# A chunk's 21 projection steps in two runs instead of five, inside a delta-rule recurrence

## The reference

```
def step(s, inp):
    r_t, w_t, k_t, v_t, kk_t, a_t = inp
    sa = einsum('bhij,bhj->bhi', s, -kk_t)
    s = s * w_t + sa (kk_t * a_t) + v_t k_t
    return s, einsum('bhij,bhj->bhi', s, r_t)
```

## Time and profile before

| what | value |
|---|---|
| median of 3 runs | 1475.15 us (1470.92 to 1475.57) |
| the profiled execution's own time | 1467.87 us |
| its span (first to last instruction) | 1466.2 us |
| TensorE busy | 1438.5 us, 98% of the span |
| VectorE busy | 837.8 us, 57% |
| ScalarE busy | 409.4 us, 28% |
| GpSimd busy | 184.5 us, 13% |
| mean granted TensorE clock | 0.997 |

### The profile page before, as it was taken

The page is one execution under the profiler, slowest core; times in us unless marked ns, Lnnn a source line. Parts: engine busy times, 40 slices in busy tenths (PEclk is TensorE's granted clock), DMA queues, the critical chain, the costliest instruction groups (busy, mean ns, idle before and its releaser), DMA issues.

```text
span 1466.2 us, 30386 instructions
## 1 busy us (share of the span) xinstructions
PE 1438.5 (98%) x12380; PEld 1138.4 (78%) x12380; DVE 837.8 (57%) x1634; ACT 409.4 (28%) x888; POOL 184.5 (13%) x256
## 2 busy tenths in 40 slices
PE   9999999999999999999999999999999999999997
PEld 8887578878888866886668668888788888888886
DVE  7665058633433446315774537677666766666664
ACT  3112372123233215216775631102211011101001
POOL 1000324532222212205001310000000000000000
PEclk9999999999999999999999999999999999999999
DMA  6222543211111247447001974422222222222221
GB/s 264 87 87 72 181 167 114 93 61 46 47 47 42 95 160 233 148 132 237 32 2 53 325 297 147 140 94 87 73 86 86 75 84 87 85 73 97 90 86 61
DMA packets 57399, 163.94 MB, mean 112 GB/s; under 512 B 7312, under 2 KB 19696, under 8 KB 55952
## 3 DMA queue, kind: packets, MB, share of 16 engines
q1 hardware_dynamic: 48608, 121.46, 25.2%
q0 software_dynamic: 7936, 39.40, 7.6%
q10 hardware_dynamic: 720, 1.16, 0.2%
HBM read 144.01 MB, written 22.15 MB: 113 GB/s over the span
## 4 chain that ended last, share of the span: by engine, by line
PE 93%; DVE 3%; ACT 1%; issue 1%; DMA 0%; SPq 0%; DVEq 0%; ACTq 0%
PE acc L1049 26%; PE acc L1194 14%; PE acc L1980 5%; PE acc L2008 5%; PE acc L1989 5%; PE acc L1219 5%; PE acc L2033 4%; PE acc L1142 2%; PE acc L1335 2%; PE acc L1157 2%; PE acc L1735 2%; PE acc L1747 2%; PE acc L1631 1%; PE acc L1758 1%; PE acc L1352 1%; PE acc L1061 1%
## 5 line engine op out<-in xcount | busy, mean ns | idle before, releaser
L1049 PE MATMUL acc<-sb_work,sb_ring 128*128 128x272 f32 x602 | 150.8, 392 | 0.0
L2530 ACT ACTIVATE sb_omemT<-acc 128x272 f32<-128x272 f32 x74 | 29.3, 396 | 386.1 <-PE acc L1980 234.5
L1049 PE MATMUL acc<-sb_work 128*128 128x272 f32 x530 | 133.0, 393 | 0.0
L1049 PEld LDWEIGHTS acc<-sb_work,sb_ring 128*128 128x128 f32 x602 | 114.4, 190 | 23.6
L1049 PEld LDWEIGHTS acc<-sb_work 128*128 128x128 f32 x530 | 100.5, 190 | 21.4 <-issue 0.8
L1194 PE MATMUL acc<-sb_work,sb_ring 128*128 128x272 f32 x360 | 93.3, 399 | 2.9 <-DVE sb_work L2739 2.9
L1194 PEld LDWEIGHTS acc<-sb_work,sb_ring 128*128 128x128 f32 x360 | 66.4, 190 | 17.9 <-issue 4.4
L1980 PE MATMUL acc<-sb_work,sb_ring 128*128 128x272 f32 x308 | 77.2, 393 | 1.0 <-issue 1.0
L1219 PE MATMUL acc<-sb_work,sb_ring 128*128 128x272 f32 x320 | 77.7, 395 | 0.0
L1989 PE MATMUL acc<-sb_work,sb_ring 128*128 128x272 f32 x308 | 77.1, 392 | 0.0
L1219 PEld LDWEIGHTS acc<-sb_work,sb_ring 128*128 128x128 f32 x320 | 59.7, 190 | 14.9 <-issue 3.3
(11 more groups left out here) (491 smaller groups left out, 2771.9 us busy)
## 6 DMA issues: line engine op xcount, KB each, us to landing
sb_ring<-w_stream SPq DMA_DIRECT2D x144, 512.0 KB, 3.5
sb_work<-pages SPq DMA_DIRECT2D x56, 192.0 KB, 4.2
branch_gates<-sb_work SPq DMA_DIRECT2D x24, 272.0 KB, 2.7
sb_work<-branch_gates POOLq DMA_DIRECT2D x8, 816.0 KB, 14.9
sb_ring<-w_stream SPq DMA_DIRECT2D x16, 384.0 KB, 3.4
sb_work<-mem_kT SPq DMA_DIRECT2D x8, 512.0 KB, 8.4
sb_work<-mem_v SPq DMA_DIRECT2D x8, 512.0 KB, 10.6
query_features<-sb_work SPq DMA_DIRECT2D x10, 272.0 KB, 3.6
```

The costliest lines, as they stand in the source:

```text
L1049: mm = pe.matmul(out, w[:, q, :], x[q], start=q == 0, stop=q == n - 1)
```

## The change

The steps planned for a chunk stay 21, and all steps stay in the same order. The places after levels 1, 2 and 3 get none; the places before `out_u` and after level 0 get 11 and 10 instead of 3 and 3.

```
         for c in range(NCH):
-            for r, n in {4: 3, 6: 3, 8: 5, 10: 5, 12: 5}.items():
+            for r, n in {4: 11, 6: 10, 8: 0, 10: 0, 12: 0}.items():
                 plan((c, r), n)
```

## The result

The changed kernel takes 1486.64 us (median of 5 runs, 1483.72 to 1494.94), the kernel before 1470.92 us beside it (median of 5, 1467.94 to 1475.57). The ratio is 1.0118 [1.0096, 1.0140], that is +17.4 us [14.1, 20.6]; it is estimated from all runs, and the two medians alone differ by 15.7.

A forecast was written before the change was run, and what follows sets the result against it. TensorE was taken to bound the recurrence. 8 x 1.11 us (longer runs less emptied places) plus 7 x 0.60 (late mask) gave +13.1, from the 1475.15 median 1488; range 1478 to 1500.

The forecast's parts named there:

- Price of a step: TensorE's projection steps (two matmul instructions each): 0.46 us a step, so 15 moved steps add 6.90 us a chunk.
- long runs cost nothing extra: Runs of 11 and 10 before `out_u` and level 1: 0.46 us a step still, as in a run of ten.
- A: Rival, runs of 11 and 10: a step is cheaper in a long run, so not slower, 1475 or 1467; chance 0.08.
- C: Rival, long runs: steps stall on their own evictions, 0.2 us in five phases a chunk, +8, 1496; chance 0.05.
- An emptied place: First `solve_x` to next `solve_y`, after levels 1 to 3: 1.42 us waiting for ScalarE's first copy, instead of 3.35.
- The last `solve_x`: Last level: VectorE's mask, behind `x_first`, makes it 0.80 us late; `out_w` returns 0.20; net +0.60 in seven chunks.
- rival B: Recurrence's short products with pauses: the clock falls, +16 us (1504) or 83 more (1571); chance 0.05.
- rival D: GpSimd meets VectorE's `x_first`: 1.52 us more in each of seven chunks, 10.6 us, 1499; chance 0.03.
- Nothing else: No cost in the sum beyond the emptied places, moved steps and VectorE's lateness at the last level.
- Other queues: Stores (SP) and GpSimd's sums wait for phases whose order is the same: taken as 0.

The follow-up runs named there:

- mask first: Changed kernel with VectorE's `x_first` for the next chunk put behind the last level's masks instead of before them: 1481.73 us, 1.0087 of the kernel before.
- shifted stream: Changed kernel with 64 more semaphore increments in TensorE's queue ahead of the recurrence, nothing else moved: 1496.44 us, 1.0201 of the kernel before.
- level 3 emptied: Against the kernel before, only the place after level 3 emptied (steps 6, 5, 5, 5, 0): 1480.55 us, 1.0082.
- level 3 kept: Against the kernel before, places after levels 1 and 2 emptied, the one after level 3 keeps five steps (8, 8, 0, 0, 5): 1476.50 us, 1.0053.
- run cut in two: Changed kernel, run of eleven split from the second chunk on, five steps before `out_w`, six before `out_u`: 1486.06 us, 1.0127 of the kernel before.

## Why the prediction was right, and what it left out

It was right in sign and range, and in the two waits that it named; 1486.64 us beside 1488. That the two lie so near is in part luck, as the terms below show. Its working against the runs:

- *Price of a step, 0.46 us; long runs cost nothing extra.* Right. 11 steps 5.24 us, no wait inside. Rivals A and C have no ground. (A's break-even with VectorE's lateness is (5.79 - 0.53) / 15 = 0.35 us a step, not 0.32; 0.46 is far from both.)
- *An emptied place is 1.42 us.* 1.47 in the profile. The copy starts 1.00 us after the first `solve_x` (0.99 was taken) and takes 0.33; the term that was small is the wake, 0.14 between ScalarE and TensorE where I took 0.10 from a VectorE row. Three places make +0.15 a chunk.
- *The last `solve_x` 4.74 us after `grams`.* Exactly so, with VectorE's queue as written. But 0.37 comes back behind it and not 0.20, because `out_w` follows sooner (0.68 us in chunk 5, 474.76 to 475.44) than the 0.86 that I took. So the net cost is 0.37 a chunk instead of 0.60: 2.6 us, not 4.2. With the 0.15 above the two misses nearly cancel: the two waits come to 12.7 us, and 13.1 was forecast.
- *Clock 1.00 (rival B).* Right for the changed kernel: 1.00, 2.4 GHz, from 303 to 545 us in both its profiles. 24 pauses of half a microsecond between short products did not lower it. The Trainium skill, "TensorE: Matmul & The Clock Gate", section "A second HAM failure mode: psum-queue depth-cycling", tells of a kernel in which frequent short idle times between groups of matmuls did; here the waits did not. In two variants the clock did fall, once, in the last chunk, after a pause on top of them: to a mean of 0.72 over 6 us with the mask first (524 to 530, after 1.3 us) and in the shifted stream. That is at most 6 x 0.28 = 1.7 us each, an estimate.
- *GpSimd and `x_first` (rival D).* Not met in the changed kernel (552 and 554 ns medians for lines 2824 and 2827). The price is real, as the version with the mask first shows, 742 ns, but that is 0.4 us a chunk and not 1.52, and there it was off the path. In the earlier trace rows the first operation took 1.45 us instead of 0.55, beside one of GpSimd's sums (line 848, 292.56 to 293.83), which is no staging copy; so 0.9 of the 1.52 came from the sum.
- *Nothing else.* This step failed: under "Other queues" the prediction took 0, and it had no term for the pauses that no semaphore ends, 4.3 and 6.0 us in two profiles. The trace of the kernel before already had three such pauses after the recurrence (0.9, 1.2 and 1.6 us, ending at 826.5, 846.4 and 851.9).

With the measured place and pauses the terms close. The steps: 0.46 for each step moved, less what the places shrink to (1.47 empty, 1.51 with one step, 1.97 with two, 3.35 with five), times 8. The mask: seven times what a chunk grows by it from `turn_v` to `from_uv`, 0.37, or 0.33 with one step; nothing with two, whose chunks take 27.62 again where no pause falls in. The pauses: all other "issue" rows of 286 to 545 us, but for the 0.7 of line 1352 that stood there before. In us:

| kernel | steps | mask | pauses | sum | measured |
|---|---|---|---|---|---|
| changed | 10.1 | 2.6 | 6.0 | 18.7 | 17.4 [14.1, 20.6] |
| changed, again | 10.1 | 2.6 | 4.3 | 17.0 | 18.8 [15.1, 22.5] |
| one step left | 0 | 2.3 | 5.1 | 7.4 | 7.3 [4.4, 10.3] |
| two steps left | 0 | 0 | 2.8 | 2.8 | 2.6 [0.3, 5.0] |
| mask first | 10.1 | 0 | 2.2 | 12.3 | 12.8 [9.7, 15.9] |
| one step, mask first | 0 | 0 | 1.4 | 1.4 | 3.2 [1.2, 5.1] |
| level 3 emptied | 3.4 | 2.6 | 3.7 | 9.7 | 12.0 [8.7, 15.4] |
| level 3 kept | 6.7 | 0 | 0.2 | 6.9 | 7.8 [5.3, 10.4] |
| run cut in two | 11.4 | 2.6 | 1.8 | 15.8 | 18.6 [15.6, 21.7] |

(The pauses are those of one execution each, and vary. For the run cut in two, steps has 7 x 0.19 for the added run.) Every sum lies within its interval. The forecast of +13.1 stands for the first two columns of the first row, which come to 12.7. The median came nearer to 1488 than the terms deserve: the forecast was set on the slower median of three runs, 1475.15 instead of 1470.92, and the pauses that it left out make up for that.

*What the pauses are.* Part 3 of the page has 99 packets of instructions, 1.62 MB, on queue 8. TensorE has 12,380 matmuls and as many weight loads, 250 for each packet, so I read that queue as TensorE's instructions, arriving in blocks of some 250. At a chunk's end `solve_x`, `out_w`, `from_uv` and `solve_first` are 168 products with as many loads, and take 3.26 us in chunk 5 (474.76 to 478.02), so a block is used up there in some 2.4 us; in a run of steps, with four such instructions in 0.46 us, one lasts 29 us. These windows of a quarter microsecond hold such a block (the last two columns: DMA share and GB/s) ahead of the pauses in chunks 1 and 3:

```profile
324.75:325.00 0.25, 0.25 (x18) 0.18 (x11) 0.00 (x0) 0.09 (x1) 0.25 (x2) 1.00 0.33 66
...
387.00:387.25 0.25, 0.25 (x14) 0.25 (x14) 0.00 (x0) 0.00 (x0) 0.25 (x1) 1.00 0.36 66
```

TensorE goes on at 327.51 and 389.87, 2.6 and 2.9 us later. That is longer than a block lasts there, and the five steps after level 3 used to stretch it.

The traces also show where the pauses stand. I count TensorE's instructions from the start of the trace: weight loads, matmuls and those that only handle semaphores. In the changed kernel the five pauses come after 3777, 5057, 6338, 12226 and 12481 of them. Divided by 256 each leaves 193 or 194 (loads overlap matmuls, so this order in time is good to one). In the shifted stream they come after 7618, 8898, 12226 and 12482: other work, and each leaves 194. The ten profiles from the changed kernel on have 35 such pauses between 303 and 545 us, and all 35 stand so; each ends 2.2 to 2.9 us after a packet of queue 8 has started. The other "issue" waits of that stretch, those for a mask, the 0.7 of line 1352 and the 8.8 behind the increments, stand at no fixed place. The three pauses of the kernel before leave 193 or 194 too. So the pauses stand at the seams between blocks of 256 instructions. That TensorE waits there for its next block is what the place and the packets together say; it is not shown by time, since the same work in fewer instructions was not tried. The stretch has some 40 seams and at most five pauses in a profile; which seams pause differs between executions of one kernel, and why stays open.

## What to carry to other kernels

A filler between two dependent steps of a chain is worth the hole it covers, not its own length: here one step of 0.46 us covers ScalarE's copy, the second VectorE's queue, and the other three bridged only the pauses, 2.6 us [0.3, 5.0] in this kernel. Emptying a place also brings every later step forward, so work out which engine's queue is late next (here VectorE, with work for the next chunk ahead of an urgent mask); the wait it made went away by reordering that queue. Where long instructions are taken out of a stretch of hundreds of very short ones, keep some allowance for pauses that no semaphore explains, and count the instructions between them: distances that are multiples of one number (256 here) tell them from waits for another engine.

## What the runs showed of the hardware

- Pauses of 0.2 to 2.0 us in stretches of short products, ended by no semaphore, 0.2 to 6.0 us a kernel: all 35 at one place in 256 of TensorE's instructions, each ending 2.2 to 2.9 us after a 16 KB instruction packet had started. 64 instructions put in front moved them to other work.
- 64 semaphore increments in TensorE's queue left it idle for 8.8 us, about 0.14 us each (in the trace they start 0.15 us apart), though the engine had nothing else to do with them. The granted clock was 0.82 in the 20 us from 300, after TensorE had been idle for 8.8 us; in the kernel before and in the changed kernel's first profile it was 1.00 there.
- The 2.3 us idle in the same place, before line 1194, left the clock at 1.00 in the kernel before and in the changed kernel's first profile. In three others (changed again, two steps, one step with the mask first) it was 0.79 from 296 to 304 us after the same idle time. So this drop, some 8 x 0.21 = 1.7 us by estimate, comes and goes between executions of one kernel; it is in none of the sums above.
- In the profiled execution of the changed kernel, and in those with level 3 emptied and kept, ScalarE stood still once, outside the recurrence, and TensorE waited for it for 4.4, 2.6 and 4.3 us (line 1509, for line 2326). No run here says why. Behind it the granted clock was 0.74 from 580 to 600 us in the changed kernel. The wait and the clock are part of why that execution was the slowest.
